# Routing and the first gather of a mixture-of-experts step, counted and gathered block by block between parts of the last output product

## The reference, cut to what matters

```python
x = x + jnp.einsum('bte,ed->btd', merged, w_out)
h2 = rmsnorm(x, ffn_norm_w)
x = x + moe_ffn(h2, ...)
# moe_ffn:
logits = jnp.einsum('td,de->te', h, w_router) + b_router
top_vals, top_idx = lax.top_k(logits, TOP_K)
gates = jax.nn.softmax(top_vals, axis=-1)
# tokens are sorted by expert; for each expert block:
u = xb @ w_up[e] + b_up[e]
a = glu * jax.nn.sigmoid(SWIGLU_ALPHA * glu) * (lin + 1)
return a @ w_down[e] + b_down[e]
# and summed back into the tokens, times the gate
```

## Time and profile before

| | |
|---|---|
| median of 3 runs | 1234.34 us (1232.02 to 1234.65) |
| the profiled execution | 1233.08 us, span 1231.3 us |
| PE busy | 1162.8 us (94%), 5421 instructions |
| DVE busy | 379.0 us (31%), 755 instructions |
| ACT busy | 142.0 us (12%), 261 instructions |
| moved by DMA | 441.88 MB, mean 359 GB/s |
| mean granted TensorE clock | 0.981 |

### The profile page before, as it was taken

The page is one execution under the profiler, slowest core; times in us unless marked ns, Lnnn a source line. Parts: engine busy times, 40 slices in busy tenths (PEclk is TensorE's granted clock), DMA queues, the critical chain, the costliest instruction groups (busy, mean ns, idle before and its releaser), DMA issues.

```text
span 1231.3 us, 13833 instructions
## 1 busy us (share of the span) xinstructions
PE 1162.8 (94%) x5421; PEld 530.8 (43%) x5421; DVE 379.0 (31%) x755; ACT 142.0 (12%) x261; POOL 16.6 (1%) x31
## 2 busy tenths in 40 slices
PE   8999999998999898989999999999999999898998
PEld 5688888653333233333333333333333334333333
DVE  3655264543223141403122222222222223140413
ACT  2122314430001010101000000000000101010100
POOL 2000001000000000000000000000000000000000
PEclk8999999998999999999999999999999999999999
DMA  9943335563889999999999999999999999999992
GB/s 306 364 146 137 119 122 176 227 238 123 361 342 430 428 427 430 428 426 430 430 426 430 430 426 429 430 427 428 430 427 428 430 428 427 430 428 427 430 429 122
DMA packets 49428, 441.88 MB, mean 359 GB/s; under 512 B 4570, under 2 KB 10810, under 8 KB 24716
## 3 DMA queue, kind: packets, MB, share of 16 engines
q1 hardware_dynamic: 47080, 434.72, 85.0%
q0 software_dynamic: 1648, 5.83, 1.6%
q10 hardware_dynamic: 676, 1.00, 0.3%
HBM read 440.23 MB, written 2.36 MB: 359 GB/s over the span
## 4 chain that ended last, share of the span: by engine, by line
PE 75%; DMA 20%; DVE 3%; issue 1%; SPq 1%; ACT 0%; DVEq 0%
PE pB L1119 33%; PE pA L1119 25%; DMA ring<-in_w_up 18%; PE pM L1119 13%; PE pM L1122 2%; DMA ring<-in_w_down 2%; PE pA L1122 2%; DVE area L1029 1%; SPq L450 1%; DMA x<-in_x_prompt 0%; DVE rt L1018 0%; DVE x L1091 0%; DVE conv_row L975 0%; DVE conv_row L972 0%; ACT hn L559 0%
## 5 line engine op out<-in xcount | busy, mean ns | idle before, releaser
L1119 PE MATMUL pA<-ring,area 128*64 128x512 f32 (+1 forms) x2080 | 492.0, 608 | 43.0 <-DMA ring<-in_w_up 43.0
L1119 PEld LDWEIGHTS pA<-ring,area 128*64 128x64 f32 (+1 forms) x2080 | 166.0, 141 | 347.5 <-issue 344.7
L1119 PE MATMUL pB<-ring,area 128*64 128x512 f32 (+1 forms) x1040 | 229.9, 594 | 1.0 <-issue 0.5
L1119 PE MATMUL pB<-area,ring 128*128 128x264 f32 (+1 forms) x928 | 185.7, 390 | 0.4 <-DVE area L732 0.4
L1119 PEld LDWEIGHTS pB<-area,ring 128*128 128x128 f32 (+1 forms) x928 | 144.7, 176 | 34.0 <-issue 3.2
L1070 DVE TENSOR_SCALAR area<-pA 128x512 f32<-128x512 f32 x32 | 22.0, 688 | 426.1 <-PE pA L1119 426.1
L1119 PEld LDWEIGHTS pB<-ring,area 128*64 128x64 f32 (+1 forms) x1040 | 73.2, 135 | 133.5 <-issue 132.0
L665 ACT ACTIVATE area<-area 128x512 f32<-128x512 f32 x32 | 20.2, 631 | 625.7 <-DVE area L1070 625.7
L1119 PE MATMUL pM<-area 128*128 128x512 f32 (+1 forms) x192 | 77.7, 610 | 4.9 <-DVE area L1029 4.9
L1082 DVE COPY area<-pB 128x512 f32<-128x512 f32 x16 | 11.1, 692 | 222.9 <-PE pB L1119 222.9
L1119 PE MATMUL pM<-hn,area 128*128 128x512 f32 x136 | 69.1, 632 | 6.8 <-DVE area L988 4.6
(11 more groups left out here) (216 smaller groups left out, 558.9 us busy)
## 6 DMA issues: line engine op xcount, KB each, us to landing
ring<-in_w_up SPq DMA_DIRECT2D x126, 2048.0 KB, 16.1
ring<-in_w_down SPq DMA_DIRECT2D x63, 2048.0 KB, 17.1
ring<-in_w_in SPq DMA_DIRECT2D x24, 1024.0 KB, 12.1
ring<-in_w_out SPq DMA_DIRECT2D x4, 1024.0 KB, 6.3
area<-in_w_up SPq DMA_DIRECT2D x2, 2048.0 KB, 14.7
area<-rev_scratch POOLq DMA_DIRECT2D x4, 512.0 KB, 7.0
area<-in_w_down SPq DMA_DIRECT2D x1, 2048.0 KB, 8.4
ring<-in_w_in SPq DMA_DIRECT2D x2, 512.0 KB, 9.0
```

The source lines that it names most:

```text
L1119: return pe.matmul(out, w, m, start=start, stop=stop, skip_group_check=True)
```

## The change

`BRANCH` has another order. The last output product, `out (1, 1)`, is cut in three parts, (0, 3), (3, 6) and (6, 8) of its eight steps of k, and the turning, logits and counting of block 0 stand between them. Counts are made in the order sample, block 0, block 1: `("count", 0)` counts the sample block and block 0 and makes `pick[:, 0]` and `s_pick`; `("count", 1)` does block 1. The split of the sample rows (`s_split`) stands before the add of `out (1, 0)` on DVE. The first gather goes into `pA` instead of `pM`, in pieces: block 0's first half after the turning of the last piece of `x`, its second half and the sample's after the logits of block 1, block 1's when its pick is made. Both `keep_busy` are gone. The totals go to a bank of `pB`, and DVE sets the flag, with a semaphore of its own, after it has copied and scaled the gathered rows. The gates, places and picks of later passes stand after that copy too. Slots of `w_out` are freed at pieces 2 and 4 instead of 1 and 2.

```diff
-BRANCH = [("out", (2, 0)), ("out", (0, 0)), ("x_cols", 0), ("rms", 2), ("out", (1, 0)), ("x_cols", 1),
-          ("logits", 2), ("out", (0, 1)), ("x_cols", 3), ("rms", 0), ("out", (1, 1)), ("x_cols", 2),
-          ("x_cols", 4), ("rms", 1), ("logits", 0), ("logits", 1)]
+BRANCH = [("out", (2, 0)), ("out", (0, 0)), ("x_cols", 0), ("rms", 2), ("out", (0, 1)), ("x_cols", 1), ("logits", 2),
+          ("s_split", 0), ("out", (1, 0)), ("x_cols", 2), ("rms", 0), ("part", (0, 3)), ("x_cols", 3), ("logits", 0),
+          ("part", (3, 6)), ("count", 0), ("part", (6, KT)), ("out", (1, 1)), ("x_cols", 4), ("rms", 1),
+          ("logits", 1), ("gather", 1), ("count", 1)]
...
# DVE
+                elif what == "count":
+                    b = misc_bank()
+                    if a == 0:
+                        V.scalar_tensor_tensor(out=t32[0:DEC, 2, :], in0=b[0:DEC, NE:2 * NE], scalar=1.0,
+                                               in1=mask[0:DEC, 2, :], op0=ALU.add, op1=ALU.mult)
+                    V.scalar_tensor_tensor(out=t32[:, a, :], in0=b[:, 0:NE], scalar=1.0, in1=mask[:, a, :],
+                                           op0=ALU.add, op1=ALU.mult).then_inc(misc_free, 1)
+                    dve.wait_ge(misc_free, misc.n)
+                    if a == 0:
+                        place = t32[:, 0, 0:2].unsqueeze(2).to_broadcast([128, 2, CAP])
+                        V.tensor_tensor(pick[:, 0], cst[:, C_IOTA + 1:C_IOTA + 1 + CAP].unsqueeze(1)
+                                        .to_broadcast([128, 2, CAP]), place, ALU.is_equal).then_inc(first_pick, 1)
+                        for j in range(3):
+                            ins = V.tensor_scalar(s_pos[32 * j:32 * j + DEC, 0:NE], t32[0:DEC, 2, :], -1.0, None, ALU.add)
+                        link(ins)
+                        s_picks(s_pos[0:96, 0:2]).then_inc(s_pick_ready, 1)
...
+            dve.wait_ge(first_pick, 1)
+            iota = cst[:, C_IOTA + 1:C_IOTA + 1 + CAP].unsqueeze(1)
+            V.tensor_tensor(pick[:, 1], iota.to_broadcast([128, 2, CAP]),
+                            t32[:, 1, 0:2].unsqueeze(2).to_broadcast([128, 2, CAP]), ALU.is_equal).then_inc(first_pick, 1)
...
+            for half in range(2):
+                dve.wait_ge(first_full, half + 1)
+                gathered(half, pA[:, 512 * half:512 * half + 512]).then_inc(first_rows, 1)
+            dve.wait_ge(fnorm_loaded, 16)
+            for half in range(2):
+                x_turned(half, misc_bank()).then_inc(misc_free, 1)
...
-            picks(t32[:, :, 0:2], 1).then_inc(pick_ready, 1)
...
+            V.tensor_tensor(pick[:, 2], iota.to_broadcast([128, 2, CAP]),
+                            t32[:, 2, 0:2].unsqueeze(2).to_broadcast([128, 2, CAP]), ALU.is_equal).then_inc(pick_ready, 1)
...
-            link(V.tensor_reduce(stat[:, 60:61], b[:, 3 * NE:4 * NE], AX.X, ALU.max))
+            dve.wait_ge(total_full, 1)
+            link(V.tensor_reduce(stat[:, 60:61], pB[:, 1, 0:NE], AX.X, ALU.max))
...
# PE
+            def first_gather(m, h):
+                return matmul(pA[:, 512 * h:512 * h + 512], pick[:, m].rearrange("p e s -> p (e s)"),
+                              hn[:, m, 512 * h:512 * h + 512], start=(m == 0), stop=(m == 1))
...
                 elif what == "x_cols":
                     b = misc_bank()
-                    pe.wait_ge(x_added, (2, 3, 5, 4, 6)[a])
+                    pe.wait_ge(x_added, a + 2)
                     mm = columns(a, x, b)
-                    if a in (1, 2):
+                    if a in (2, 4):
                         mm.then_inc(ring_free, 1)
+                    if a == 4:
+                        pe.wait_ge(first_pick, 1)
+                        pe.wait_ge(hn_ready, 2)
+                        first_gather(0, 0)
...
+                elif what == "gather":
+                    first_gather(0, 1)
+                    pe.wait_ge(s_parts_ready, 1)
+                    pe.wait_ge(s_pick_ready, 1)
+                    for h in range(2):
+                        matmul(pA[:, 512 * h:512 * h + 512], s_pick[0:96].rearrange("p e s -> p (e s)"),
+                               s_parts[0:96, 512 * h:512 * h + 512], start=False, stop=False)
+                elif what == "count":
+                    b = misc_bank()
+                    if a == 0:
+                        pe.wait_ge(mask_ready, 2)
+                        matmul(b[0:DEC, NE:2 * NE], count_w[0:DEC, 0, 0:DEC], mask[0:DEC, 2, :])
+                    else:
+                        pe.wait_ge(mask_ready, 3)
+                    matmul(b[:, 0:NE], count_w[0:DEC, 1, :], mask[0:DEC, 2, :], stop=False)
+                    if a == 1:
+                        matmul(b[:, 0:NE], count_w[:, 1, :], mask[:, 0, :], start=False, stop=False)
+                    matmul(b[:, 0:NE], count_w[:, 0, :], mask[:, a, :], start=False).then_inc(misc_full, 1)
+
+            for m in (2, 0, 1):
+                rs = TOK[m][1]
+                mm = matmul(pB[:, 1, 0:NE], count_w[0:rs, 1, :], mask[0:rs, m, :], start=(m == 2), stop=(m == 1))
+            mm.then_inc(total_full, 1)
+            pe.wait_ge(first_pick, 2)
+            pe.wait_ge(hn_ready, 3)
+            for h in range(2):
+                first_gather(1, h).then_inc(first_full, 1)
...
             for half in range(2):
                 b = misc_bank()
-                pe.wait_ge(misc_free, FILL["gather", half])
+                pe.wait_ge(first_rows, half + 1)
                 x_turn(b, half)
```

More of the change, by code:

```diff
@@ L166 @@
 COLS = [(2, 0, 8), (0, 0, 4), (0, 4, 4), (1, 0, 4), (1, 4, 4)]
[L169 to L174 removed]
+BRANCH = [("out", (2, 0)), ("out", (0, 0)), ("x_cols", 0), ("rms", 2), ("out", (0, 1)), ("x_cols", 1), ("logits", 2),
+          ("s_split", 0), ("out", (1, 0)), ("x_cols", 2), ("rms", 0), ("part", (0, 3)), ("x_cols", 3), ("logits", 0),
+          ("part", (3, 6)), ("count", 0), ("part", (6, KT)), ("out", (1, 1)), ("x_cols", 4), ("rms", 1),
+          ("logits", 1), ("gather", 1), ("count", 1)]
+FILLS_OF = {"tile": 0, "square_in": 0, "split": 0, "qknorm": 0, "scores": 0, "bias": 0, "exp": 0, "norm": 0, "turn": 0, "s_norm": 0, "out": 0, "rms": 0,
+            "s_split": 0, "part": 0, "gather": 0}
 FILL, _n = {}, 0
[L176 removed]
+for _s in STEPS + BRANCH + [("x_turn", 0), ("x_turn", 1)]:
     _n += FILLS_OF.get(_s[0], 1)
@@ L484, in _ @@
             store(PRE_FILLS + PAIR_FILLS * PAIRS)
+            sp.wait_ge(flag_ready, 1)
             over = sp.value_load(flag[0:1, 0:1], min_val=0, max_val=1)
@@ L1019, in _ @@
                                     ALU.add)
-            link(V.tensor_reduce(stat[:, 60:61], b[:, 3 * NE:4 * NE], AX.X, ALU.max))
+            dve.wait_ge(total_full, 1)
+            link(V.tensor_reduce(stat[:, 60:61], pB[:, 1, 0:NE], AX.X, ALU.max))
             link(V.tensor_scalar(flag_f32[:], stat[0:1, 60:61], float(CAP), None, ALU.is_gt))
[L1022 to L1036, removed]
+            V.tensor_copy(flag[0:1, 0:1], flag_f32[:]).then_inc(flag_ready, 1)
             misc0 = misc.n
@@ L1288, in _, with out_part @@
             pe.wait_ge(tile_free_act, ACT_TILES[len(TILES)])
-            norms = 0
+            def out_part(a, n, k0, k1):
+                w = ring[:, (W_IN_CHUNKS + n) % SLOTS, :].rearrange("p (k n) -> p k n", k=KT)
+                t0, r = TOK[a]
+                o = 1024 * a + 512 * n
+                for k in range(k0, k1):
+                    mm = matmul(pA[:, o:o + 512], yc[:, k, t0:t0 + r], w[:, k], start=(k == 0), stop=(k == KT - 1))
+                return mm
+            def first_gather(m, h):
+                return matmul(pA[:, 512 * h:512 * h + 512], pick[:, m].rearrange("p e s -> p (e s)"),
+                              hn[:, m, 512 * h:512 * h + 512], start=(m == 0), stop=(m == 1))
             for what, a in BRANCH:
@@ L1308, in _ @@
                         continue
[L1309 to L1312, removed]
+                    if (a, n) != (1, 1):
+                        out_part(a, n, 0, KT).then_inc(out_full, 1)
+                elif what == "part":
+                    mm = out_part(1, 1, *a)
+                    if a[1] == KT:
+                        mm.then_inc(out_full, 1)
                 elif what == "x_cols":
                     b = misc_bank()
-                    pe.wait_ge(x_added, (2, 3, 5, 4, 6)[a])
+                    pe.wait_ge(x_added, a + 2)
                     mm = columns(a, x, b)
-                    if a in (1, 2):
+                    if a in (2, 4):
                         mm.then_inc(ring_free, 1)
+                    if a == 4:
+                        pe.wait_ge(first_pick, 1)
+                        pe.wait_ge(hn_ready, 2)
+                        first_gather(0, 0)
                 elif what == "logits":
@@ L1364, in x_turn @@
                 mm.then_inc(misc_full, 1)
[L1366 to L1371, removed]
-                    pe.wait_ge(s_parts_ready, 1)
-                    pe.wait_ge(s_pick_ready, 1)
-                gather_sample(*part)
```

(3 more changed lines are left out.)

74 lines of the change are left out of this document (33 added, 41 removed).

## The result

Beside the prediction four executions of each kernel were timed: the changed one took 1218.36 us (1217.52 to 1220.04), the one before 1233.53 (1232.02 to 1234.65). The ratio is 0.9879, with a 95% interval of 0.9862 to 0.9897, so 15 us faster, between 12.7 and 17.0. The forecast was 1222.0 in a range of 1219 to 1226: the direction is right, the gain of 12.2 was too small, and the median lies 0.6 us under the range.

The account below looks back on a forecast made before the run. Weights bound the kernel from about 354 us, with PE's start of pair 0 setting when their stream begins. The 1231.3 span plus 1.8, less 12.2, gives 1220.9; with 1.3 to the median, 1222.0, range 1219 to 1226.

Parts of the forecast that it names:

- The bound and the start: Weights bound the kernel from about 354 us; before that transfers hang on PE, so pair 0 d us earlier ends it d earlier.
- The rival of the hidden start: Bytes loaded ahead, not PE, fix the end, so all gain is hidden and the time is 1234; chance 0.04.
- late slots: Rival: chunks for `w_out`'s slots, issued up to 8 us later, stall PE in pair 0, ending slower; chance 0.03.
- The sum of 13.26 us: Last output product's end (265.90) to pair 0: 13.26 us instead of 25.44, so pair 0 starts at 279.2.
- covered with 0.4 to spare: DVE work of `count 0`, 1.3 us, runs under the last product's final part, 1.72 us, less 0.2 for the way.
- the split: Sample rows' split on DVE, 5.73 us, before the add of `out (1, 0)`: ends at 259.3, slack 1.7 us.
- the logits: Logits of block 0 and of block 1 on PE, 1.88 us each in the sum.
- the pick of one block: Step from block 1's count to its gather: one pick on DVE, about 0.29 us.
- The falling clock: Rival: short waits between 268 and 279 us lower the clock, giving 3.5 us back, so 1225.6; chance 0.12.
- the step to the median: Profiled execution forecast at 1220.9; the median of the runs is 1.3 above, so 1222.1, rounded 1222.0.
- The last pair's term: Clock falls in the last pair after a wait or not, worth 1.7 us; if it no longer falls, 1220.4.
- the smallest rounding 1219: Lower end of the range, put below the 1220.4 for a last pair whose clock no longer falls.

## Why the prediction was wrong, point by point

**The bound and the start: right.** PE's start of pair 0 sets the stream, and everything behind it moved with it, to 12.33 us in the last pair. The rival of the hidden start is out; late slots too, for all chunks had landed by 281 us.

**The sum of 13.26 us: right to 0.2.** It put pair 0 at 279.2, and it started at 279.04. That it came so near is in part luck: single terms were off by up to 0.2 both ways (the selection of block 1 to the count took 1.93 for 1.78, the first piece of the gather 0.86 for 0.95). `count 0` was covered with 0.4 to spare; the split ended at 259.2 and the add began at 259.26, piece 3 being turned at 261.54; the logits took 1.72 and 1.71 where I had 1.88; the pick of one block 0.29 or 0.30, as estimated. PE's longest idle time was 0.87 us. The formula of the Trainium skill, "VectorE: DVE Perf Modes", section on the TRN2 errata, was thus rightly applied: by it the pick of one block takes 0.291.

**The falling clock: the rival did not come,** in three traces of the changed kernel and three more with matmuls added elsewhere. But the reason that I gave, that no wait is over 0.9 us, does not suffice: in one execution of an experiment the clock fell though no wait just before it was over 0.44 us, and in another kernel behind a wait of 1.14.

**What failed is the step to the median.** Its terms can be set against what was measured. The forecast for the profiled execution was 1220.9; it took 1219.10, less by 1.7 for the last pair, whose clock did not fall, and by 0.1 for the start. Then "The median of the runs is 1.3 above it" took a fixed offset from one profiled execution and three runs (1220.9 and 1.3 are 1222.2, by the way, not 1222.1); with four runs the kernel before has its median 0.45 above its profiled execution, and the changed one 0.74 below. So the 3.6 us between 1222.0 and 1218.36 are 1.8 in the profiled execution and 1.8 in the step from it. The last pair's term was there with its right size, 1.7, but "with the smallest rounding 1219" made the range's lower end out of it alone, with the offset still on top.

Missing from the range was the first stage: it ends at 231.6 to 234.9 us over the traces, a spread of 3 us that moves the whole kernel, and I had read nothing of it. Between the two first profiled executions it makes no difference (233.24 and 233.17). For the others of the changed kernel there is an estimate: the lowest, 1217.52 with a span of 1215.6, fits an issue at 231.5 and a last pair at full clock (1215.6 less 45.87 and 938.2), both favourable at once. The range should have reached 1.5 to 3 us lower and higher on that account. The draw of four executions has a share too: the two later sets have medians of 1219.82 and 1219.71, and all twelve 1219.4, which lie inside the range.

**What stays open.** By all executions the gain is 13.9, give or take 0.8, against 12.3 for the start. In the traces of the unedited kernels the remainder has two parts. The last pair's clock fell in two of three executions of the changed kernel and in two of two before, which makes about 0.6; and by the issue the first stage ended 1.4 us earlier in the three of the changed kernel (mean 232.2) than in the two of the one before (233.7). The traces of the edited kernels speak for chance in both. Their first stage is the same code, and over all traces without added warming its end is at 233.1 us on average in eight with the old order (231.8 to 234.1) and at 233.0 in seven with the new one (231.6 to 234.9). And where no matmuls were added in the pairs, the last pair's clock fell in two of six traces of the old order and in four of five of the new one, so not more often in the old. With the 12.5 us between the kernels whose last pair kept its clock in every trace this makes a second gain of the change unlikely, but it does not exclude it: the untraced executions may hold something else, such as a clock in the old order's hole that costs more than in its traces.

**A better version.** The changed kernel with the matmuls in the pairs gave 1218.50, against 1218.36 to 1219.82 for the changed kernel. In the kernel before they bring 1.3 us (0.1 to 2.5); for the changed one, some 0.9 us by the means, no gain could be told from the scatter.

## What to carry to other kernels

Where a stream of weights is bound by transfers, but begins only when one engine frees the first slots, look for the stretch without transfers and shorten the chain into it: a microsecond there is one at the end. Removing one of two DVE chains in front of two waits leaves a hole of about 4 us before the other wait, and the clock falls in it all the same; both together brought 10.8 us where each alone brought 4.4. Put pieces of a large product between small steps that wait for another engine, not the whole before or after them, and give a range the spread of the stages that one did not look at.

## What the runs showed of the hardware that was not expected

The granted clock fell without a long wait: in one execution to 0.50 at 270 us with no PE idle time over 0.44 us just before it, among turnings and 32-column products, while the same instructions kept 1.00 in eight other traces; and in another kernel at 260 to 268 us (mean 0.57) around waits of 1.14 and 1.94. In the steady pairs it fell behind waits of 2.3 to 2.7 us in two or three pairs out of five, in a regular order that begins at another pair in each execution; with 1.28 us of wait left it did not fall. From 10 to 20 us one and the same code ran at 0.50 to 0.83 of the clock, and the end of the first stage moved with it by up to 3 us, and the end of the kernel with that.
